# Expert gates through a table in memory: slot weights added by indirect transfers and read back tile by tile, where one-hot matmuls made them before

## What is computed

```python
s = jnp.einsum('thpc,hpnc->thpn', q, sub_keys)          # 8 heads, 2 sides, 128 keys each
top_s, top_i = lax.top_k(s, 16)
cand_s = top_s[:, :, 0, :, None] + top_s[:, :, 1, None, :]
best_s, best_j = lax.top_k(cand_s, 16)                   # 16 slots for each token and head
g = softmax(best_s)
a = gelu(einsum('thkd,td->thk', u_sel, hb))              # u row of each selected expert
out = einsum('thk,thkd->td', g * a, v_sel)               # v row of each selected expert
```

## Time and profile before

| | |
|---|---|
| median of three runs | 3490.18 us (3485.67 to 3502.23) |
| the profiled execution, its own time | 3475.47 us |
| its span, first to last instruction | 3473.8 us |
| TensorE busy | 3424.0 us, 99% of the span |
| VectorE, ScalarE, GpSimd busy | 76%, 60%, 3% |
| granted TensorE clock, mean | 0.998 |
| DMA, mean | 208 GB/s |

### The profile page before, as it was taken

One profiled execution on the slowest core, in us unless ns is written; L12 is line 12 of the kernel. 1 busy time (PEld: TensorE's weight loads), 2 busy tenths in 40 slices (PEclk: granted clock), 3 DMA queues, 4 the chain that ended last, 5 costly groups with the idle time before them and its releaser, 6 DMA issues.

```text
span 3473.8 us, 81372 instructions
## 1 busy us (share of the span) xinstructions
PE 3424.0 (99%) x29900; PEld 3372.6 (97%) x29900; DVE 2642.9 (76%) x4896; ACT 2071.1 (60%) x3852; POOL 108.4 (3%) x169
## 2 busy tenths in 40 slices
PE   7999999999999999999999998999999999999999
PEld 7999999999999999999999997999999999999999
DVE  7875688788888888656688877999667686666655
ACT  5456655677767777555555556665565665555554
POOL 1000030000000000000000000000000000000000
PEclk9999999999999999999999999999999999999999
DMA  8854488566655555576799974555466666666665
GB/s 328 326 190 151 144 296 300 163 187 183 185 182 169 166 167 165 166 220 193 268 340 337 338 262 141 177 166 162 142 184 191 189 189 195 193 193 193 194 193 181
DMA packets 184778, 721.46 MB, mean 208 GB/s; under 512 B 20512, under 2 KB 23072, under 8 KB 171808
## 3 DMA queue, kind: packets, MB, share of 16 engines
q1 hardware_dynamic: 167328, 608.57, 55.4%
q0 software_dynamic: 14496, 103.82, 8.4%
q10 hardware_dynamic: 2784, 6.78, 0.5%
HBM read 714.89 MB, written 4.19 MB: 207 GB/s over the span
## 4 chain that ended last, share of the span: by engine, by line
PE 95%; DVE 3%; ACT 1%; issue 0%; DMA 0%; SPq 0%; DVEq 0%; ACTq 0%
PE PS L474 23%; PE PS L480 23%; PE PS L479 23%; PE PS L619 7%; PE PS L629 7%; PE PS L627 7%; PE PS L872 1%; DVE wlo L1709 1%; DVE big L1703 0%; PE PS L921 0%; PE PS L723 0%; DVE big L1636 0%; PE PS L671 0%; PE PS L910 0%; PE PS L841 0%
## 5 line engine op out<-in xcount | busy, mean ns | idle before, releaser
L1061 ACT ACTIVATE whi<-raw 128x512 fp32r<-128x512 f32 x1864 | 1157.7, 629 | 979.0 <-PE PS L480 644.6
L1563 DVE TENSOR_TENSOR wlo<-raw,whi 128x512 fp32r<-128x512 f32 x1480 | 996.7, 690 | 528.3 <-ACT whi L1061 523.5
L474 PE MATMUL PS<-tok_parts_hi,whi 128*128 128x256 f32 x2048 | 578.6, 283 | 0.9 <-ACT big L1271 0.7
L480 PE MATMUL PS<-tok_parts_hi,wlo 128*128 128x256 f32 x2048 | 573.0, 280 | 0.0
L479 PE MATMUL PS<-tok_parts_lo,whi 128*128 128x256 f32 x2047 | 572.8, 280 | 0.0
L619 PE MATMUL PS<-whi,ev_parts_hi 128*128 128x256 f32 x2048 | 565.9, 276 | 1.8 <-issue 1.8
L629 PE MATMUL PS<-whi,ev_parts_lo 128*128 128x256 f32 x2048 | 566.1, 276 | 0.0
L627 PE MATMUL PS<-wlo,ev_parts_hi 128*128 128x256 f32 x2045 | 565.0, 276 | 0.0
L1709 DVE TENSOR_TENSOR wlo<-raw,whi 128x512 fp32r<-128x512 f32 x564 | 381.9, 695 | 132.6 <-ACT whi L1149 86.0
L1149 ACT ACTIVATE whi<-raw 128x512 fp32r<-128x512 f32 x436 | 270.9, 629 | 253.7 <-PE PS L480 252.7
L480 PEld LDWEIGHTS PS<-tok_parts_hi,wlo 128*128 128x128 f32 x2048 | 390.9, 191 | 0.0
(11 more groups left out here) (562 smaller groups left out, 8111.0 us busy)
## 6 DMA issues: line engine op xcount, KB each, us to landing
raw<-peer_u_dram SPq DMA_DIRECT2D x256, 512.0 KB, 3.6
raw<-peer_v_dram SPq DMA_DIRECT2D x256, 512.0 KB, 4.3
raw<-w_in_dram SPq DMA_DIRECT2D x240, 512.0 KB, 3.8
big<-w_mod_dram POOLq DMA_DIRECT2D x96, 1024.0 KB, 6.2
raw<-w_up_dram SPq DMA_DIRECT2D x176, 512.0 KB, 3.9
raw<-w_down_dram SPq DMA_DIRECT2D x88, 512.0 KB, 4.3
raw<-w_out_dram SPq DMA_DIRECT2D x64, 512.0 KB, 4.2
raw<-w_query_dram SPq DMA_DIRECT2D x32, 512.0 KB, 5.2
```

The costliest lines, as they stand in the source:

```text
L474: pe.matmul(out, hi, rhi, start=start, stop=False, **more)
L480: return pe.matmul(out, lo, rhi, start=False, stop=stop, **more)
L1061: f(whi[:, m % PAIRS, quarter(q)], raw[:, m % RING, quarter(q)], ACT.Copy).then_inc(hi_ready, 1)
L1563: dv.tensor_tensor(wlo[:, m % PAIRS, quarter(q)], raw[:, m % RING, quarter(q)], whi[:, m % PAIRS, quarter(q)], ALU.subtract).then_inc(lo_r ...
```

## The change

Slots become addresses. For each slot VectorE computes (j * 128 + i) * 256 + token, and GpSimd adds the slot's weight to that float of a table of 128x128x256 floats in memory (`gates`, 16.8 MB), with 16 indirect transfers of 128 elements for each unit. The table is zeroed first, in 16 transfers of 1 MB out of a tile of zeros, beside the attention of the first block. Once all 256 adds have landed, GpSimd reads the table back by tiles of 128x256 (128 KB, two buffers, where `causal` lies), multiplies each into its `ga` tile, and ScalarE waits for that (`gated`) before it takes the tile in `peer_v`. All one-hot work, the turning over and the end part are gone. The loads of the late modulation rows stand in GpSimd's program among the gate tiles, each six tiles behind the step where its slot comes free. The loops of `peer_u` get a cut in chunk 1 of turns 1 to 17.

```diff
 (constants, GpSimd)
+            s.link(pool.memset(zeros, 0.0))
+            s.link(pool.iota(token, pattern=[[P, 2]], base=0, channel_multiplier=1, ...))
 (beside the first block's heads, GpSimd)
+                for n in (2 * h - 4, 2 * h - 3) if h >= 2 else ():
+                    pool.dma_start(d["gates"][8 * n:8 * n + 8].rearrange("j p t -> p j t"),
+                                   zeros.unsqueeze(1).to_broadcast([P, 8, SEQ])).then_inc(gates_zeroed, 16)
 (after the last row of the third modulation part, GpSimd)
-            pool.wait_ge(gates_done, BESIDE)
+            gates_flat = d["gates"].rearrange("j p (t o) -> (j p t) o", o=1)
+            pool.wait_ge(gates_zeroed, 16 * 16)
+            for u in range(2 * HEADS):
+                pool.wait_ge(picks_done, 2 * u + 2)
+                if u > 0:
+                    pool.wait_ge(gates_added, 16 * TOPK * u)
+                for n in range(TOPK):
+                    pool.indirect_dma_start(gates_flat, bass.IndirectOffsetOnAxis(ap=pick_at[:, u, n:n + 1], axis=0),
+                                            pick_weight[:, u, n:n + 1], None, compute_op=ALU.add).then_inc(gates_added, 16)
+            pool.wait_ge(gates_added, 16 * TOPK * 2 * HEADS)
+            def fetch_gates(n):
+                pool.dma_start(gate_tile[n % GATE_TILES], d["gates"][(n + 112) % N_SUB]).then_inc(gate_in[n % GATE_TILES], 16)
+            def gate(n):
+                j = (n + 112) % N_SUB
+                pool.wait_ge(gate_in[n % GATE_TILES], 16 * (n // GATE_TILES + 1))
+                pool.wait_ge(banks_free, 4 + 88 + j + 1)
+                pool.tensor_tensor(ga[:, j, :], ga[:, j, :], gate_tile[n % GATE_TILES], ALU.mult).then_inc(gated, 1)
+                if n + GATE_TILES < N_SUB:
+                    pool.wait_ge(gated, n + 1)
+                    fetch_gates(n + GATE_TILES)
+            for n in range(N_SUB + 8):
+                if n < N_SUB:
+                    gate(n)
+                for m in range(3 * KC):
+                    if LATE_AT[m] == n - 6:
+                        late_row(m)
 (TensorE)
-            dense("peer_u", 88, SEQ, (1, GATED // 4))
+            dense("peer_u", 88, SEQ, (1, 17), cuts=(1,))
             mod_turn(2, 7)
-            ... transposes, gates_beside in turns 17 to 31, gate_sums ...
-            pe.wait_ge(gates_used, 4 + SEQ // 4)
+            dense("peer_u", 88, SEQ, (17, 18), cuts=(1,))
+            dense("peer_u", 88, SEQ, (18, N_SUB // 4))
+            pe.wait_ge(banks_free, 4 + 216)
             spread_tokens("peer_v", N_SUB // 4, 0, (10, 14, 20))
 (ScalarE)
-            gelu_out(64, (GATED - 64) // 4)
-            ... rows_one, late_gelu, rows_end ...
+            gelu_out(64, 15)
+            sc.wait_ge(gates_added, 16 * TOPK * 2 * HEADS)
+            gelu_out(124, 1)
+                            if name == "peer_v":
+                                sc.wait_ge(gated, g * 4 + (k + 2))
 (VectorE, end of a routing unit)
+                link(dv.scalar_tensor_tensor(small_t[:, 9, :], small_t[:, 8, :], float(P), small_t[:, 7, :], ALU.mult, ALU.add))
+                dv.tensor_scalar(pick_at[:, u, :], small_t[:, 9, :], float(SEQ), token[:, half:half + 1],
+                                 ALU.mult, ALU.add).then_inc(picks_done, 1)
                 dv.wait_ge(best_exp, u + 1)
                 link(dv.reciprocal(small[:, 27:28], small[:, 7:8]))
-                link(dv.tensor_scalar(small_t[:, 9, :], best, small[:, 27:28], None, ALU.mult))
-                for c in range(3):
-                    move(sel8[:, c, u, :], small_t[:, 7 + c, :]).then_inc(picks_done, 1)
+                dv.tensor_scalar(pick_weight[:, u, :], best, small[:, 27:28], None, ALU.mult).then_inc(picks_done, 1)
-            ... picked, hot_parts, hot_cols, apply_gates, gate_late ...
```

More of the change, by code:

```diff
@@ L321, in build @@
         sx_copied = sem("sx_copied")
[L322 to L325, removed]
+        row_ready, best_ready, best_exp, picks_done = (sem("pk_" + n) for n in "row best exp done".split())
+        gates_zeroed, gates_added, gated = (sem("g_" + n) for n in "zeroed added gated".split())
+        gate_in = [sem(f"gate_in{s}") for s in range(GATE_TILES)]
         causal_again = sem("causal_again")
@@ L435, in _ @@
                                base=META, pattern=[[P, 2], [-1, KEYS]], channel_multiplier=1).then_inc(causal_again, 1)
[L436 to L454, removed]
-                    pool.wait_ge(modw_used, part * KC + kc + 1)
-                    pool.dma_start(modring_late[:, kc % MOD_RING, :],
-                                   d["w_mod"][part * KC + kc]).then_inc(modw_in[kc % MOD_RING], 16)
             pool.wait_ge(stage_lo, N_SUB)
@@ L480, in three, with dense @@
                 return pe.matmul(out, lo, rhi, start=False, stop=stop, **more)
-            def dense(name, chunk0, width, turns=None, inputs=None):
+            def dense(name, chunk0, width, turns=None, inputs=None, cuts=()):
                 first, n = turns or (0, dict(STREAM)[name] // 8)
@@ L1965, in _ @@
-                for c in range(3):
-                    move(sel8[:, c, u, :], small_t[:, 7 + c, :]).then_inc(picks_done, 1)
-            keep_mod_rows(2, 7)
-            with dv.Fori(16, GATED // 4) as g:
-                for k in range(4):
-                    split(g, FIRST["peer_u"], 2 * k + 2)
+                dv.tensor_scalar(pick_weight[:, u, :], best, small[:, 27:28], None, ALU.mult).then_inc(picks_done, 1)
+            with s.loop(HEADS, 27) as u:
+                route_turn(u, 0)
+            with s.loop(2 * HEADS, 27, first=HEADS) as u:
+                route_turn(u, 1)
@@ L1971, in _, with splits @@
+            keep_mod_rows(2, 7)
+            def splits(turns):
+                with dv.Fori(*turns) as g:
+                    for k in range(4):
+                        split(g, FIRST["peer_u"], 2 * k + 2)
+            splits((16, 17))
             dv.wait_ge(mod_summed, 2)
             link(add_mod(MOD_EARLY * KC, KC, 7))
-            dv.memset(small[:, 26:27], 0.0).then_inc(gates_used, 4)
-            dv.wait_ge(picks_turned, 6)
-            for n in range(6):
-                dv.tensor_copy(picked[:, n % 3, (n // 3) * P:(n // 3 + 1) * P],
-                               PS[:, 4 + n // 4, (n % 4) * P:(n % 4 + 1) * P]).then_inc(picks_ready, 1)
```

142 lines of the change are left out of this document (22 added, 120 removed).

## The result

The changed kernel takes 3437.89 us, the median of four runs (3422.36 to 3451.97), beside 3490.20 for the kernel before on the same chip (3485.67 to 3502.23): the ratio is 0.9854, with an interval of 0.9827 to 0.988. It is faster, by 52 us where 64 were forecast, and inside the range. The profiled execution took 3437.23 us.

A forecast was written before the change was run, and what follows sets the result against it. TensorE, busy 99% of the span, was taken to bound the kernel. Terms -51 - 6 - 9.8 + 3 = -64, taken from the median 3490, gave 3426 us, range 3408 to 3478.

The forecast's parts named there:

- Turns 17 to 31, -51: In `peer_u` after routing: 60 chunks of 6.30 us become 15 dense turns of 21.76 at the fast pace, -51 us.
- Rival 1: The slow pace stays or comes back in turns 18 to 31, routing gives nothing back: -46, 3444 us; chance 0.16.
- Routing turns, -6: Turns 2 to 16 of `peer_u`: a cut in chunk 1 shortens each from 22.60 to 22.23 us, -6 in all.
- Between the products, -9.8: From the last gate matmul to the first of `peer_v`: the gap of 11.6 us shrinks to 1.8, so -9.8.
- The adds, free: GpSimd's 256 indirect transfers at 1.1 us each, 20.5 a unit, keep up with routing and cost nothing below 2.4 each.
- Rival 4: The adds come too late: beyond 2.4 us each, ScalarE stops at turn 31; gain gone from 2.65; chance 0.05.
- Rival 3: An add holds VectorE in routing; from 0.27 us each the gain is gone, at 0.53 3556 us; chance 0.08.
- rival 5: The adds fill the DMA engines: beyond 68 ns an element weights come late; gain gone at 100 ns; chance 0.06.
- Zeroing, free: 16 transfers of 1 MB beside the heads lift DMA from 147 to 240 GB/s and cost nothing.
- `peer_v`, +3: Reading the table back and multiplying on GpSimd beside VectorE in `peer_v` was allowed +3 us over the whole.
- rival 2: `peer_v` no longer hidden: port or DMA contention lengthens turns 14 to 29 by 1 to 2 us, +16 to +32; chance 0.11.
- It fits narrowly: In `peer_v` from turn 14, four GpSimd multiplies hold VectorE at most 3.0 us of its 3.5 idle a turn.

## Why the prediction was right, and where its sizes were off

The direction and the range held, and so did the mechanism of the large terms: matmuls taken off TensorE, and the gap closed. What did not hold is the rule under the pace, that a hitch starts the slow one and a cut ends it. It was made from one hitch and one cut. By the prediction's own steps:

1. **Turns 17 to 31, -51: right.** From the cut in turn 17 at 1023.3 to the last matmul at 1343.1 are 319.8 us for 58.8 chunks, 5.44 each, as forecast. Rival 1 (the slow pace) did not come here; the kernel without cuts shows that it would have: its `peer_u` was 13.7 us longer, where the rival's working has 12 for turns 18 to 31 and 6 for routing. The fast pace here was no luck, nine profiles of nine had it behind this cut.
2. **Routing turns, -6: half of it.** A turn is 22.41 us and not 22.23. The working had one hitch a turn; there are two or three, in one turn five, and VectorE, which waits 5.1 us in 270, still sets the turn. It is -3, and the kernel before with cuts gains as much (759.5 for 763.1). Here too the rule was too simple: the slow pace ended at hitches as well as at cuts, and ran on behind one cut of the changed kernel (866.5).
3. **Between the products, -9.8: -9.0.** The term left out VectorE's `gmod` step of 0.70 us, which now stands between the last `wlo` and the remainder that TensorE waits for. It had been hidden in the old 11.6.
4. **The adds, free: right, with less room.** 1.55 us each and 35.6 us a unit where 1.1 and 20.5 were taken. So "it keeps up with routing" was wrong, a turn being 22.4; what saved the term is the deadline at turn 31, which left some 90 us. The add is inside the bounds given. Rival 4's place was right (the adds made twice stop TensorE there and nowhere else). Rival 3 is excluded by the `wlo` steps, 690 and 689 ns, and rival 5 by 51 ns an element, both confirmed by the run with one add.
5. **Zeroing, free: right.** 0.90 us an issue and 239 GB/s as worked out, no matmul lost.
6. **`peer_v`, +3: the step that was too small.** It cost 12.8 in the profile. Both parts of rival 2 are real and show separately: the multiplies hold VectorE 0.62 us each, so 2.5 a turn in which it had 3.5, and the reads make weights late. "It fits narrowly" looked at means; a late landing and a locked quarter in the same chunk don't. What this costs directly is near the +3: the holes over 0.15 us in TensorE's starts hold 5.0 us more than the pace, where the kernel before has 0.3. The larger part, the other 8, is pace: 212 us of slow pace between 1689 and 1911, begun at a hitch of 0.19 us, at 3.8% are 8.1. The prediction knew from turn 1 that a hitch can start the slow pace, and used it for the gain, but not to price a stall in `peer_v`. Nor is the 8 a fixed price of the change: the same sum is 1 us with the gates ahead, 9 with no gate work beside the product, 19 in the changed kernel without cuts, and 5 to 6 for the kernel before with all cuts. That it was 8 in this profile is partly chance.
7. **Outside the sum:** `w_down` +9.1 and 3.4 ahead of `peer_u`. The second goes with two dips of the granted clock to the 1.2 GHz level, at 194 and 222 us, before zeroing begins at 259. In 180 to 256 us TensorE has 537 matmuls at a mean of 0.96, and 560 at 1.00 in the kernel before. Ahead of the first dip it was held back in both kernels alike, 18 matmuls in 4 us (190 to 194):

```profile
194.00:198.00 4.00, 4.00 (x21) 4.00 (x21) 2.31 (x8) 0.63 (x1) 0.50 (x1) 0.57 0.91 315
```
```profile
194.00:198.00 4.00, 4.00 (x34) 4.00 (x33) 2.70 (x8) 1.26 (x2) 0.16 (x1) 1.00 0.80 276
```

   The first line is the changed kernel, the second the kernel before. The prediction said that the profiled execution lay 15 under the median, but took its difference as spread over everything; 9 of it was one stage in its lucky pace. Starting from the median was right for that reason.

Terms as measured: -51 - 3 - 9 + 12.8 = -50, and the medians say -52. The agreement is looser than it looks: the terms come from two single executions, whose `peer_v` alone can differ by ten us through the pace, and the four runs of the changed kernel spread over 30 us.

What stays open: why ScalarE still waits 28 to 45 us for the stream where all gate reads are over by 1647; 22 of those 37 waits lie behind 1850, where the queue carries nothing that the kernel before doesn't. Three profiles of kernels without a table range from 9.5 to 20.2, so some of it is spread. Also open is why one hitch or cut changes the pace and the next doesn't, and whether the dips of the clock ahead of `peer_u` have to do with the change: the mean clock of 180 to 256 us was below 1.00 in six of ten profiles with a table (0.96 in three, 0.98 in three) and in none of three without.

## What to carry to other kernels

Read a pace from counts in a window for every stage, also for those that a change doesn't touch: two executions of the same instructions can differ by 9 us in one stage, and a difference of profiles is then no price of the change. Where an engine that sets the end has a slow pace that a short hole can start, price a stall as a range, from the hole alone to the hole plus a slow stretch, and try on the chip what ends such a stretch. And before you say that a measure ended it, look at the pace just ahead of the measure: in `w_down` here all three kernels with added cuts were fast, and had been so before the first of these cuts. When a helper engine takes over work, its total may be far inside its deadline, as here 256 adds are, while the small part that it must do beside a nearly full VectorE costs more than all the rest.

## What the runs showed of the hardware

- An indirect add of 128 elements holds GpSimd for 1.55 us, 1.86 from one start to the next with the 0.30 between; landing 3.3 us at the median where one stood alone. It doesn't lengthen two-input steps on VectorE (690 against 689 ns).
- A GpSimd multiply of 128x256 beside VectorE's `wlo` steps costs them 0.62 of its 0.75 us. One of 128x1 takes GpSimd 0.49 us on average over the product (median 0.34) and 0.72 on average in its busy part, and costs VectorE's steps nothing that shows (687 to 691 ns).
- TensorE has two paces at a granted clock of 1.00, 113.3 and 117.7 ns for 256 columns. The pace changes at hitches, where a start comes some 0.05 to 0.3 us late, and at cut pairs, either way, and not at each of them: the slow one ended at the cut in turn 17 of `peer_u` in 9 of 9 profiles and at cuts in `peer_v` in 9 of 15 meetings, it began behind the opening cut of `w_down` in 7 of 13, and it ended seven times with no cut in the routing turns of the kernel without cuts.
- A half of 512 KB that landed late took 10.86 us (in the chain, 1849.68 to 1860.54) in a stretch with a DMA share of 0.94, where 4.3 is the median before.
